# State-space heads with clamped exponents and paired products, and the Fourier products moved between the gate products

## What is computed

```python
def ssd_scan(xd, da, bm, cm, h0):                 # 16 heads in 4 groups, head width 64, state 128, chunks of 128
    a_cs = jnp.cumsum(da, axis=2)
    seg = jnp.where(lower, a_lr[..., :, None] - a_lr[..., None, :], -jnp.inf)
    cb = jnp.einsum('bclgn,bcsgn->bcgls', cm, bm)
    y_diag = jnp.einsum('bcgrls,bcsgrp->bclgrp', cb[:, :, :, None] * jnp.exp(seg), xd)
    ...
    y_off = jnp.einsum('bcqgn,bcgrpn->bcqgrp', cm, h_in) * jnp.exp(a_cs)[..., None]

def ssd_mixer(z, xbc, dt_raw, ...):
    y_f, h_f = ssd_scan(xs * dt[:, :, 0, :, None], da[:, :, 0], bm, cm, h0_f)
    y_b, h_b = ssd_scan(flip(xs * dt[:, :, 1, :, None]), flip(da[:, :, 1]), flip(bm), flip(cm), h0_b)
    y = y_f + flip(y_b) + d_skip[:, None] * xs
    y = y.reshape(b, l, D_SSD) * jax.nn.silu(z)
    return rmsnorm(y, norm_w), h_f, h_b

def fourier_mixer(f, w_four):                     # 4 groups of 128 channels
    spec = jnp.fft.fft2(fg, axes=(1, 3), norm='ortho').real
    return jnp.einsum('blgc,gcd->blgd', spec, w_four)

x = x + g1 * (jnp.concatenate([y_l, fourier_mixer(f_l, w_four)], axis=-1) @ w_out)
x = x + g2 * hier_moe(modulate(rmsnorm(x, norm2), sh2, sc2), ...)
```

## Time and profile before

| | us |
|---|---|
| median of three runs | 1679.51 |
| the profiled execution, its own time | 1678.7 |
| its span, first to last instruction | 1676.6 |
| TensorE busy | 1557.7 (93%) |
| VectorE busy | 729.7 (44%) |
| ScalarE busy | 564.0 (34%) |
| mean granted TensorE clock | 0.978 |

### The profile page before, as it was taken

One profiled execution on the slowest core, in us unless ns is written; L12 is line 12 of the kernel. 1 busy time (PEld: TensorE's weight loads), 2 busy tenths in 40 slices (PEclk: granted clock), 3 DMA queues, 4 the chain that ended last, 5 costly groups with the idle time before them and its releaser, 6 DMA issues.

```text
span 1676.6 us, 22456 instructions
## 1 busy us (share of the span) xinstructions
PE 1557.7 (93%) x9476; PEld 1176.6 (70%) x9476; DVE 729.7 (44%) x1102; ACT 564.0 (34%) x813; POOL 46.7 (3%) x41
## 2 busy tenths in 40 slices
PE   7999999999998999999799978695999999999996
PEld 7898989999896889999444855485444454444543
DVE  5568657664593467753344547403111111111112
ACT  5543464444646364444522224303011011111112
POOL 2000010000220010000000000000000000000000
PEclk9999999999999999999899989997999999999999
DMA  9552564554656464555412500041699999999991
GB/s 380 193 199 101 202 251 156 196 186 171 255 185 235 174 230 173 201 172 208 174 50 85 200 24 0 4 151 50 270 421 414 423 413 422 423 412 423 413 423 72
DMA packets 27852, 382.92 MB, mean 228 GB/s; under 512 B 3152, under 2 KB 3280, under 8 KB 4480
## 3 DMA queue, kind: packets, MB, share of 16 engines
q1 hardware_dynamic: 27072, 377.71, 57.5%
q0 software_dynamic: 704, 4.11, 0.6%
HBM read 380.76 MB, written 1.05 MB: 228 GB/s over the span
## 4 chain that ended last, share of the span: by engine, by line
PE 57%; DVE 5%; ACT 4%; issue 2%; DMA 1%; POOL 0%; DVEq 0%; ACTq 0%; POOLq 0%
PE ps L518 48%; PE ps L926 4%; PE ps L935 4%; ACT HM L995 2%; DVE HM L1352 1%; DVE HM L1340 1%; ACT work L995 1%; ACT L995 1%; DVE work L1340 1%; DVE w_lo L1340 1%; DMA work<-in_ctx 1%; PE ps L655 0%; PE ps L974 0%; PE ps L968 0%; DVE work L1352 0%
## 5 line engine op out<-in xcount | busy, mean ns | idle before, releaser
L1340 DVE TENSOR_TENSOR w_lo<-ring,w_hi 128x1024 fp32r<-128x1024 f32 x220 | 282.3, 1288 | 209.6 <-ACT w_hi L995 209.5
L518 PE MATMUL ps<-ring,work 128*64 128x512 f32 x1536 | 336.9, 594 | 15.5 <-ACT work L995 15.5
L518 PE MATMUL ps<-in_hi,w_hi 128*128 128x256 f32 x1152 | 328.7, 285 | 20.9 <-DVE w_lo L1340 15.6
L518 PE MATMUL ps<-in_hi,w_lo 128*128 128x256 f32 x1152 | 325.4, 282 | 0.0
L518 PE MATMUL ps<-in_lo,w_hi 128*128 128x256 f32 x1152 | 325.2, 282 | 0.0
L995 ACT ACTIVATE w_hi<-ring 128x1024 fp32r<-128x1024 f32 x220 | 231.8, 1056 | 240.2 <-PE ps L518 223.9
L518 PEld LDWEIGHTS ps<-ring,work 128*64 128x64 f32 x1536 | 121.6, 137 | 211.0 <-issue 211.0
L995 ACT ACTIVATE work<-ps 128x512 f32<-128x512 f32 (+2 forms) x132 | 77.8, 629 | 554.1 <-PE ps L518 307.0
L518 PEld LDWEIGHTS ps<-in_hi,w_hi 128*128 128x128 f32 x1152 | 218.8, 190 | 27.1 <-issue 19.9
L518 PEld LDWEIGHTS ps<-in_lo,w_hi 128*128 128x128 f32 x1152 | 218.9, 190 | 0.1
L518 PEld LDWEIGHTS ps<-in_hi,w_lo 128*128 128x128 f32 x1152 | 218.8, 190 | 0.0
(11 more groups left out here) (195 smaller groups left out, 1647.1 us busy)
## 6 DMA issues: line engine op xcount, KB each, us to landing
ring<-in_experts SPq DMA_DIRECT2D x96, 2048.0 KB, 11.3
ring<-in_dense SPq DMA_DIRECT2D x82, 2048.0 KB, 8.4
ring<-in_dense SPq DMA_DIRECT2D x4, 512.0 KB, 8.1
cst<-in_ret_cst POOLq DMA_DIRECT2D x1, 1280.0 KB, 13.3
X<-in_x SPq DMA_DIRECT2D x4, 256.0 KB, 7.1
cst<-in_ssd_cst POOLq DMA_DIRECT2D x1, 1024.0 KB, 5.1
work<-in_ctx POOLq DMA_DIRECT2D x1, 1024.0 KB, 8.8
out<-HM SPq DMA_DIRECT2D x1, 1024.0 KB, 3.8
```

Source lines behind the costliest of these rows:

```text
L518: i = pe.matmul(o, l, r, start=start, stop=stop)
L1340: i = dve.tensor_tensor(out=o, in0=x, in1=y, op=op)
```

## The change

Names of new semaphores and buffers are left out where they only follow. The parts:

- Order of the projection: f before z, and z cut into four tiles of 16 products with the Fourier products between them. The Fourier products write their intermediate to work and cst, and their weights are loaded earlier, into act2.
- nega is gone. The exponent is made by ScalarE straight from the row tile, as Relu(key's decay - row), four instructions; one Exp of 768 columns with scale -1 follows. The mask becomes 0/1 and is multiplied once per group into cbx, which has two buffers.
- dt is multiplied into copies of x (xf, xb; four instructions of 1024 columns on VectorE). The four scalar_tensor_tensor instructions of a head become one tensor_tensor of 768 columns.
- decm and ce have four buffers. y is made for two heads at a time, the instructions of the two heads alternating, which write rows 0 to 63 and 64 to 127 of one tile.
- The squares of y are taken and summed inside the head loop, two tiles at a time.
- mix_out starts with its 32 products over the Fourier tiles, then the last sums of squares, then the 64 over y. Its weights are laid out to match (_mix_blocks).

```diff
-_tiles("ssd_z", 4)
 _tiles("ssd_f", 2)
-_tiles("dt_tok", 1)
+for _item in (("ssd_z", 0), ("dft", 0), ("dft", 3), ("ssd_z", 1), ("dt_tok", 0), ("dft", 1), ("dft", 4), ("dft", 6), ("dft", 9),
+              ("ssd_z", 2), ("dft", 2), ("dft", 5), ("dft", 7), ("dft", 10), ("ssd_z", 3), ("dft", 8), ("dft", 11)):
+    _seq.append(_item)
...
-    for h in range(SH):
-        if h + 2 < SH:
-            if (h + 2) % 4 == 0:
-                yield "cb", (h + 2) // 4
-            yield "row", h + 2
-        yield "y", h
+    for pair in range(SH // 2):
+        if pair + 1 < SH // 2:
+            if pair % 2:
+                yield "cb", (pair + 1) // 2
+            yield "row", 2 * pair + 2
+            yield "row", 2 * pair + 3
+        yield "y", pair
...
+        decm = at(0, 4, 768, of=flat_hm)
+        ce_at = [at(3072 + 512 * i, 512, of=flat_hm) for i in range(2)] + [at(512 * i, 512, of=flat_cst) for i in range(2)]
+        xf, xb = xs_tok[:, 0:2, :], xs_tok[:, 2:4, :]
+        cbx = at(0, 2, 2, 384)
...
# TensorE
             gemm("ssd_f", "ssd_f", FG, KD, lambda c: hcat[:, c, T:2 * T])
-
+            pe.wait_ge(s["ld_ssd"], 16)
+            pe.wait_ge(s["conv_ready"], KX + 2 * KB)
+            gate_tile(0)
+            dft_in(0)
+            dft_in(1)
+            gate_tile(1)
             t = TILE["dt_tok", 0]
...
+            dft_tokens(0)
+            dft_tokens(1)
+            dft_in(2)
+            dft_in(3)
+            gate_tile(2)
+            pe.wait_ge(s["ld_wfour"], 16)
+            dft_out(0)
+            dft_out(1)
+            dft_tokens(2)
+            dft_tokens(3)
+            gate_tile(3)
+            dft_out(2)
+            dft_out(3)
...
+                    pe.wait_ge(s["m_ready"], 2 * i + 2)
+                    for part in range(6):
+                        for h in (2 * i, 2 * i + 1):
...
+                            mm(bank(t)[rows, cols], x, y, part == 0, part == 5,
+                               bank_full[t % ROT] if part == 5 and h % 2 else None)
+                    if i % 2 and i > 1:
+                        y_sums(i // 2 - 1)
...
+            for b in range(KD * (KX + FG)):
+                c, m = (KX + b // KD, b % KD) if b < KD * FG else ((b - KD * FG) % KX, (b - KD * FG) // KX)
...
+                if b == KD * FG:
+                    y_sums(3)
...
# ScalarE, per head
-                if h >= 2:
-                    act.wait_ge(s["m_ready"], h - 1)
-                fn(act2[:, h % 2, :], bank(t), ACT.Exp, s["ea_ready"])
...
-                    fn(dm[:, j, 0:mid], rm[:, j, 0:mid], ACT.Exp, bias=nega[:, j, h:h + 1])
-                    fn(dm[:, j, mid:384], rm[:, j, mid:384], ACT.Exp, s["dec_ready"] if j == 1 else None,
-                       bias=nega[:, j, SH + h:SH + h + 1])
+                if h >= 4:
+                    await_full(act, TILE["y", h // 2 - 2])
+                dm = decm[:, h % 4, :]
                 for j in range(2):
                     mid = T - j * P
+                    fn(dm[:, j * 384:j * 384 + mid], bank(t)[:, j * P:T], ACT.Relu, scale=-1.0, bias=tok6[:, j, h:h + 1])
+                    fn(dm[:, j * 384 + mid:(j + 1) * 384], bank(t)[:, T:T + (j + 1) * P], ACT.Relu, s["rl_ready"] if j else None,
+                       scale=-1.0, bias=tok6[:, j, SH + h:SH + h + 1])
+                if h >= 2:
+                    act.wait_ge(s["ce_ready"], h - 1)
+                fn(act2[:, h % 2, :], bank(t), ACT.Exp, bank_read[t % ROT])
+                act.wait_ge(s["rl_ready"], h + 1)
+                fn(dm, dm, ACT.Exp, s["dec_ready"], scale=-1.0)
+                if h >= 7 and h % 4 == 3:
+                    y_square(h // 4 - 1)
+            y_square(3)
...
# VectorE
-            await_full(dve, TILE["ssd_f", 1])
+            await_full(dve, TILE["ssd_z", 3])
             for d in range(2):
                 for tau in range(2):
                     w16 = tok6[:, 4 + tau, d * SH:(d + 1) * SH].unsqueeze(2).to_broadcast([P, SH, SP_])
                     tt(cut(xw[:, 2 * d + tau, :], SH, SP_), cut(xs_tok[:, tau, :], SH, SP_), w16, MUL, s["xw_ready"])
+
+            dve.wait_ge(s["xw_ready"], 4)
+            for d, x in ((0, xf), (1, xb)):
+                for tau in range(2):
+                    w16 = tok6[:, 2 + tau, d * SH:(d + 1) * SH].unsqueeze(2).to_broadcast([P, SH, SP_])
+                    tt(cut(x[:, tau, :], SH, SP_), cut(xb[:, tau, :], SH, SP_), w16, MUL, s["xd_ready"])
...
+            masked(0)
+            from_state(0)
             for h in range(SH):
+                if h + 1 < SH:
+                    if (h + 1) % 4 == 0:
+                        masked((h + 1) // 4)
+                    from_state(h + 1)
...
                 dve.wait_ge(s["dec_ready"], h + 1)
+                dm = decm[:, h % 4, :]
+                tt(dm, dm, cbx[:, h // 4 % 2].rearrange("p a b -> p (a b)"), MUL, s["m_ready"])
+                if h % 2 == 0 and h >= 4:
+                    y_out(h // 2 - 2)
+            y_out(KX - 2)
             y_out(KX - 1)
```

More of the change, by code:

```diff
@@ L822, in _, with y_sums @@
                            bank_full[t % ROT] if d == 1 and tau == 1 else None)
+            def y_sums(j):
+                pe.wait_ge(s["sq_ready"], 4 * 6 + j + 1)
+                for c in range(2):
+                    mm(ps[:, STAT, 0:T], ones[:, :], ysq[j][:, c * T:(c + 1) * T], j == 0 and c == 0, j == 3 and c == 1,
+                       s["stats_full"] if j == 3 and c == 1 else None)
             pe.wait_ge(s["wt_ready"], KX + 2 * KB)
@@ L848, in _ @@
[L848 to L885, removed]
+                    pe.wait_ge(s["m_ready"], 2 * i + 2)
+                    for part in range(6):
+                        for h in (2 * i, 2 * i + 1):
+                            rows, lo = slice(h % 2 * SP_, (h % 2 + 1) * SP_), h % 4 * SP_
+                            head = slice(h * SP_, (h + 1) * SP_)
+                            dm, state_of = decm[:, h % 4, :], h0[:, h // 4, :]
+                            x, cols, y = (
+                                (xf[:, 0, head], slice(0, T), dm[:, 0:T]),
+                                (xb[:, 0, head], slice(0, P), dm[:, T:T + P]),
+                                (xf[:, 1, head], slice(P, T), dm[:, 384:384 + P]),
+                                (xb[:, 1, head], slice(0, T), dm[:, 384 + P:768]),
+                                (state_of[:, lo:lo + SP_], slice(0, T), ce_at[h % 4][:, 0:T]),
+                                (state_of[:, 256 + lo:256 + lo + SP_], slice(0, T), ce_at[h % 4][:, T:2 * T]))[part]
+                            mm(bank(t)[rows, cols], x, y, part == 0, part == 5,
+                               bank_full[t % ROT] if part == 5 and h % 2 else None)
@@ new lines, in _ @@
+                    if i % 2 and i > 1:
+                        y_sums(i // 2 - 1)
+            for j in range(4):
+                await_room(pe, TILE["mix_out", j])
+            for b in range(KD * (KX + FG)):
+                c, m = (KX + b // KD, b % KD) if b < KD * FG else ((b - KD * FG) % KX, (b - KD * FG) // KX)
+                t = TILE["mix_out", m // 2]
+                if b % BPU == 0:
+                    w = weights("mix_out", b // BPU)
+                if b == KD * FG:
+                    y_sums(3)
+                if m == 0:
+                    if c < KX:
+                        pe.wait_ge(s["h_ready"], KD * 2 + c + 1)
+                    else:
+                        await_read(pe, TILE["dft", 3 * (c - KX) + 2])
+                last = c == KX - 1 and m % 2 == 1
+                mm(bank(t)[:, m % 2 * T:(m % 2 + 1) * T], w[:, b % BPU * P:(b % BPU + 1) * P], mix[:, c, :],
+                   c == KX and m % 2 == 0, last, bank_full[t % ROT] if last else None)
```

170 lines of the change are left out of this document (92 added, 78 removed).

## The result

The changed kernel takes 1668.95 us (four runs, 1667.87 to 1670.5) against 1679.63 us in the same runs of before: ratio 0.9934, 95% interval 0.9917 to 0.9952. That is 10.7 us less; a second set of runs of the same kernel, further down, gave 10.1. I had forecast 17.0 less, 1662.5, with 1651 to 1675 as the range.

What follows compares the result with a forecast made beforehand. TensorE fills the experts; ahead of them, 122 us of stages hold 32 us without TensorE. mix_out starting 27.6 us earlier, less 3.8 inside it and 6.8 for clock, gives 17.0 less: 1662.5 us, range 1651 to 1675.

Steps and rivals of the forecast that it cites:

- Experts unchanged: Experts stage, 486 us, full of TensorE at clock 1.00: keeps its length, so time saved ahead counts whole.
- States 10.4 later: Projection to states: Fourier products and transposes moved ahead make the states start at 988.8 instead of 978.42.
- ScalarE, VectorE: Head loop, work per head: ScalarE 2.77 us (four Relu 1.35, two Exp 0.57 and 0.85), VectorE 2.4 us.
- Relu: ScalarE in the head loop: four Relu 1.35 us; by the skill's rule up to 3.9 a head, shrinking the gain by 18.
- rival (e): ScalarE in the head loop: Relu and Exp need separate tables, two loads of 1.28 us a head; 1687 us; chance 0.06.
- y side by side: TensorE in the head loop: y of two heads overlaps, taking 2.4 us a pair instead of 4.6.
- rival (d): Head loop: the two heads' y don't overlap, 17.6 us back, fewer clock drops; 1674 us; chance 0.06.
- The ring: Head loop: ce, product, y, row, Relu, Exp in sequence set the pace, 7.3 us a pair; six turns 43.8 plus 4.9 extras.
- mix_out: Inside mix_out: last sums 0.9 us and 2.9 of waiting for the norm, together 3.8 us more than before.
- The clock: Head loop: TensorE's clock falls in four turns of seven at 1.7 us, costing 6.8; loop clock about 0.85.
- rival (b): Head loop: the clock falls in every turn, costing 14.3 us with cb and sums; 1670 us; chance 0.10.
- the first heads: States to the end of Exp of row 2: 11.0 us to row 0 full, then 8.7 us.

Runs made afterwards that it cites:

- one head at a time: The changed kernel with all six products of a pair's even head before those of the odd one, not alternating: 1680.01 us, ratio to before 0.9989.
- with fillers: The changed kernel with five useless 256-column products on TensorE ahead of each wait for m_ready in the head loop: 1660.32 us, ratio to before 0.9888.
- rows ahead: The changed kernel with rows and cb of the pair after next ahead of y in TensorE's order: 1657.23 us, ratio to before 0.9864.
- sums early: The changed kernel with the last sums of squares after 8 instead of 32 of mix_out's products over the Fourier tiles: 1667.18 us, ratio to before 0.9932.
- two fillers: The changed kernel with two useless products instead of five ahead of each wait for m_ready: 1663.62 us, ratio to before 0.9887.
- the Fourier part alone: The kernel before with only the change's Fourier part, head loop as before, squares and sums after the loop: 1672.99 us, ratio to before 0.9958.
- Fillers ahead of it: The changed kernel with rows ahead, sums early and useless products in TensorE's waits, those behind mix_out included: 1635.5 us, ratio to before 0.9729.

## Why the prediction held, and which term was off

- **Experts unchanged**: 486.43 against 486.30 us. Right.
- **States 10.4 later**: from the end of the C product to the states 61.8 us (930.10 to 991.88) against 51.1 (927.36 to 978.42), 10.7 later, with a wait of 3.96 (3.9 in the sum) and the low clock after it kept (8.83 against 9.16). The products of dt ran beside the states. Right.
- **ScalarE, VectorE**: four Relu 1.35, Exp of 768 columns 0.83 (0.85), product of 768 columns 0.95 (0.95), ce 0.69 (0.66). The durations are right, but an instruction starts before the one ahead has ended: start to start Relu takes 1.23 and ce 0.61, and a head on ScalarE 2.42 (1006.62 to 1009.04) instead of the 2.77 summed.
- **Relu**: the prediction drew a price of up to 3.9 us from the Trainium skill. Its rule ("ScalarE: Activation LUTs", Rules for kernel authors) sends relu to VectorE as the faster engine, with a figure for bf16; it doesn't say that Relu takes longer than other functions on ScalarE, so that price was a misreading, and 1.35 us doesn't refute the rule. No run here has Relu on VectorE. One table serves Relu and Exp, as the Trainium skill says in the Table sets section of the same page: the trace agrees, with no load between 1004.10 and 1080.83, and rival (e) is out. (The 22 us that the prediction adds to (e) count one switch a head, where (e) has two loads; it should have been 44.)
- **y side by side**: 2.31 us at full clock (2.4). Right, and rival (d) is out. The run with one head at a time is a milder case of (d): it cost 10.0 us in the stage, not 17.6, since part of the overlap stays in that order. Yet by its ratio it stands at 1678, 4 us over (d)'s 1674, which counted on fewer drops; none went.
- **The ring**: 6.97 us at full clock (7.3), 8.02 with cb or sums; six turns 48.6 us with fillers, where the prediction had 43.8 + 4.9 = 48.7. The mechanism is right, and shown twice: by the fillers and by taking the rows out of the ring. That the two sums meet is partly luck: wholly at full clock the turns would take 6.97 + 5 x 8.02 = 47.1, since the links were 0.3 a turn too long, and a first turn at the low level made up for it.
- **mix_out**: a wait of 2.81 (2.9) and 0.9 of sums as summed, but 5.6 us longer than before in all, not 3.8 (47.03 against the 41.44 from 1094.59 to 1136.03): the wait dropped the clock, 128 records took 29.54 us where 0.217 each make 27.8. A term of 1.8 was missing.
- **The clock, the term that was mis-sized.** "Four turns of seven at 1.7: 6.8" should have been every turn: six turns took 59.5 us where the sum at full clock had 48.7, 10.8 more (and 12.4 more than the 47.1 above). The granted clock of the stage was 0.72, not about 0.85; the prediction's own last paragraph names a clock under 0.75 as a sign of being wrong. The case that came is rival (b), a drop in every turn, which had a chance of 0.10. That its 1670 lies so near 1669 is partly luck: it priced the loop at 14.3 us, too much, and left out the two terms that follow. The failing step was the evidence: I weighed one wait of 2.76 us in the Fourier stretch that left the clock up against drops after 4.48, and 1.93 with 1.25, and took the middle. In the loop the wait comes back in every turn; that the repetition is what matters was not tested by itself.
- **Not in the sum**: the norm and routing behind mix_out took 0.8 us more than before (37.47 against 36.68, 1136.03 to 1172.71), by the clock.

So 17.0 became 10.7. The turns were 4.0 worse than allowed (10.8 instead of 6.8), mix_out 1.8, the routing 0.8, the states 0.3, and the first heads 0.8 better (18.9 us instead of 19.7 from the states to the end of the Exp of row 2): 6.1 in all, near the 6.3 that are missing. The chances favoured faster, and it was faster. The forecast's own band, 1657 to 1668, missed by 1 us; the range held, with the mechanism right except for how often the clock falls.

## What to carry to other kernels

When instructions of several engines form a ring with a fixed order, sum the ring, not the engines: none of the three was busy for more than 76% of the loop (TensorE 50.9 of 67.4 us), and moving short products ahead of their consumer in one engine's list was worth more (11.7 us) than the whole rewrite of the heads (3 to 4). Price every recurring wait of TensorE at the low clock unless a row shows the same wait, repeated, at full clock; where it can't be removed, products without use in it pay for themselves. And look behind the stage for what the clock takes back.

## What the runs showed of the hardware that I had not expected

- A wait of 2.75 us in a turn of some 10 came with a drop of the granted clock in every one of six turns, in two profiles; in two of the six the clock fell only after y had begun (16 records in 1.78 us at 1062.41). With 0.3 us left of the wait the stage had 0.97. With 1.6 us left, three of six turns had y wholly or mostly low (2.83, 2.50, 2.40) and three high (1.52), in turns with the same work. With the rows ahead, one y came at full clock after 2.90 us.
- Two 64-column products in the two halves of the array cost exactly one (2.31 us for 24 records and for 12), narrow 128-column parts included. With one head after the other only the products on either side of the seam still overlapped, an estimated 3.7 us a pair.
- Shortening one stage lengthened an untouched one: the routing product of 32 narrow records took 4.15 us in the changed kernel and 6.88 in four single edits ahead of it (five fillers, rows ahead, one head at a time, sums early); in the runs with two fillers and with the Fourier part alone it took 4.09 and 4.04. It follows the level that the clock has when it comes; what sets that I didn't separate. Fillers ahead of it gave 3.66.
